# The order of the attention units: row block inside head, and one score product per step

## The chip, the cores and the metric

The kernel runs on one core of a Trainium2 chip. The metric is the device time of one execution in microseconds (us); lower is better.

## The reference

The reference is two transformer blocks on 256 tokens of width 2048, batch 1, in float32. The change lies in the second block, in its sparse attention, whose input projection and attention read

```python
h = rms_norm_2(x, ln_mix_pre[l])
z = h @ w_in[l]
q, kv, nsa_gl, u, merge_logits = jnp.split(z, splits, axis=-1)
q = q.reshape(b, s, NSA_HEADS, HEAD_DIM)               # 16 heads of 64
kv = kv.reshape(b, s, 6, NSA_GROUPS, HEAD_DIM)         # 4 groups of keys and values
a = nsa_attention(q, kv[:, :, 0], ..., kv[:, :, 5], nsa_gl, ...)
# in nsa_attention, for each block of 128 queries and each head, float32:
s_s = einsum(q, k_sel) * scale + bias;  p_s = masked_softmax(s_s);  o_s = p_s @ v_sel
s_w = einsum(q, k_win) * scale + bias;  p_w = masked_softmax(s_w);  o_w = p_w @ v_win
out = gate_c * o_c + gate_s * o_s + gate_w * o_w
```

With 256 tokens every selection block and the whole window are in reach, so both softmaxes run over all keys up to the query: 128 keys for the first block of queries (r = 0) and 256 for the second (r = 1).

## The kernel before

All engines are programmed by hand: each has one list of instructions, in an order written out in Python, and they meet through semaphores. There is no scheduler.

**Weights.** A weight slab of 1 MB (4 tiles of 128 rows by up to 512 columns) goes by DMA into one of four `raw` buffers. ScalarE writes its rounded part to `wh` (`hi`), VectorE the remainder to `wl` (`lo`, L1722), two buffers each, and TensorE multiplies it as 24 float32r matmuls: 2 row blocks, 4 tiles, 3 products (`slab_mm`, L1098 to L1100).

**The stage of the change.** Forty-eight steps m. In step m TensorE multiplies slab m of the second block's input projection (`z2_slab`); the attention on columns already there runs between the slabs. There are 32 units, one for each head and query block; unit u starts in step u + 12 (`STEP_U`). In one step TensorE does, in this order: the slab; the scores of a unit (`scores`, L1537, one float32 product of Q transposed with the selected and the window keys together, 2 x 128 columns out for r = 0 and 2 x 256 for r = 1); the transposes of the probabilities of unit u - 2 (`prob_turn`, L1572, 2 blocks for r = 0, 4 for r = 1); the products with the values for unit u - 3 (`weighted`, L1589 and L1591).

A head has 64 dimensions, so the score product contracts over 64 partitions. `par` says which half: the queries and keys of a unit with par = 0 lie in partitions 0 to 63, those with par = 1 in 64 to 127 (`QT`, `KT2`). A float32 product is two instructions for TensorE, here called passes.

VectorE does in step m: `biased(u)` (adds the bias L2217 by the helper at L1720, row maximum L2220, its negative L2221), then `lo` of slab m + 2, then `gathered(u - 3)` (L2273 to L2284). ScalarE does `hi` of slab m + 2, `prob_out(u - 2)` (L948) and the exponentials of unit u (`probs`).

Before the change the units go in the order (r, par) = (0,0), (0,1), (1,0), (1,1) for each i. The scores of two units stand back to back in every second step:

```python
if 0 <= u < UNITS and u % 2 == 0:
    scores(u)
    scores(u + 1)
```

The unit with even u writes bank 2, the one with odd u bank 3.

Of the kernel before, what the change touches and what calls it, by code (L numbers as in the profile page):

```python
# [23 lines left out]
SEQ, D, RB = 256, 2048, 2  # L24
# [37 lines left out]
UNITS = NH * RB  # L62
# [8 lines left out]

def unit(u):

    i, r, par = u // 4, (u % 4) // 2, u % 2
    return 8 * (i // 4) + 4 * par + i % 4, i, par, r

XH, XD = 4, 128
# [130 lines left out]
def build(nc, A, out):  # L208
    ctx = ExitStack()
    with ctx:  # L210
        named = {}

        def S(name):
            if name not in named:
                named[name] = ctx.enter_context(nc.semaphore(name))
            return named[name]
# [147 lines left out]
        def QT(i, par, r):  # L364

            c0 = 256 * (i % 4) + P * r
            return Z2[HD * par:HD * par + HD, i // 4, c0:c0 + P]

        def KT2(g, n):

            return Z2[HD * (g % 2):HD * (g % 2) + HD, g // 2, Z2_KV + 512:Z2_KV + 1536].rearrange("p (b c) -> p b c", b=2)[:, :, 0:n]
# [203 lines left out]
        def _(act):  # L575
            st = Slabs()

            def f(out_, in_, func, name, **kw):
                act.activation(out_, in_, func, **kw).then_inc(S(name), 1)  # L579
# [361 lines left out]

            def prob_out(u):

                nb = 2 + 2 * unit(u)[3]
                act.wait_ge(S("n_turned"), u + 1)
                if u >= 2:
                    act.wait_ge(S("n_pv"), u - 1)
                f(pT[:, u % 2, 0:nb * P], PB[4][:, 0:nb * P], ACT.Copy, "npT_out")  # L948
# [8 lines left out]
            for m in range(STEPS):  # L957
# [32 lines left out]
                u = m - STEP_U  # L990
# [62 lines left out]
        def _(pe):  # L1053
# [407 lines left out]
            def z2_slab(m):  # L1461

                n, s = 4 + m // 4, m % 4
                evacuated = RB * (CHUNK0["zin2"] + n - 1)
                if n == 4 and s == 0:
                    pe.wait_ge(chunk_out, evacuated)
                slab_mm((0, 1), ALL[4 * s:4 * s + 4], Z2_PARTS[n // Z2N][1], s == 0, s == 3, half=s == 3,
                        row_free=evacuated if s == 0 and n > 4 else None)

            def raw_turn(b):  # L1470

                pe.wait_ge(chunk_out, RB * (CHUNK0["zin2"] + 4))
                if b == 3:
                    pe.wait_ge(S("pe_out"), 1)
                for k in range(2):
                    for r in range(RB):
                        c0 = Z2_KV + KVW * (b // 2) + HD * (2 * (b % 2) + k)
                        cols = slice(SEQ * k + P * r, SEQ * k + P * r + P)
                        pe.transpose(PB[4 + b][0:HD, cols], Z2[:, r, c0:c0 + HD], ident)
                        mm = pe.matmul(PB[4 + b][HD:2 * HD, cols], Z2[:, r, c0:c0 + HD], ident, start=True, stop=True)  # L1480
                mm.then_inc(S("raw_turned"), 1)

            def hidden_w1(k):

                pe.wait_ge(S(f"w1_in{k}"), 32)
                pe.wait_ge(S("raw_out"), 4)
                for l in range(CS):
                    mm = pe.matmul(PB[4 + k][:, 0:NG * NCMP].rearrange("p (g n) -> p g n", g=NG), w1s[k][:, l, :],
                                   rawT[k][:, :, l:l + CS * (NCMP - 1) + 1:CS], start=l == 0, stop=l == CS - 1)
                mm.then_inc(S("w1_used"), 1)  # L1490

            def compressed():

                pe.wait_ge(S("gelued"), 2)
                for par in range(2):
                    mm = pe.matmul(PB[6][HD * par:HD * par + HD, 0:NG // 2 * NCMP].rearrange("p (q n) -> p q n", q=NG // 2),
                                   w2s[:, 0, :], hidT[:, 0, :].rearrange("p (q g n) -> p g q n", g=2, n=NCMP)[:, par, :, :],
                                   start=True, stop=True)
                mm.then_inc(S("kc_done"), 1)
                for g in range(NG):  # L1500
                    mm = pe.matmul(PB[7][0:NCMP, HD * g:HD * g + HD], hidT[:, 1, NCMP * g:NCMP * g + NCMP], w2s[:, 1, :],
                                   start=True, stop=True)
                mm.then_inc(S("kc_done"), 1)

            def query_turn(p):

                pe.wait_ge(S("kc_out"), 2)
                for j in range(4):
                    i = 4 * p + j
                    for r in range(RB):  # L1510
                        cols = slice(SEQ * (i % 2) + P * r, SEQ * (i % 2) + P * r + P)
                        low, high = (Z2[:, r, HD * h:HD * h + HD] for h in (8 * p + j, 8 * p + 4 + j))
                        pe.transpose(PB[4 + i // 2][0:HD, cols], low, ident)
                        mm = pe.matmul(PB[4 + i // 2][HD:2 * HD, cols], high, ident, start=True, stop=True)
                    if i % 2:
                        mm.then_inc(S("nq_turned"), 1)

            def key_turn():

                pe.wait_ge(S("nq_out"), 4)  # L1520
                pe.wait_ge(chunk_out, RB * (CHUNK0["zin2"] + 6))
                for p in range(2):
                    for b in range(2):
                        for r in range(RB):
                            c0 = Z2_KV + 512 * (1 + b) + P * p
                            mm = pe.transpose(PB[4 + p][:, SEQ * b + P * r:SEQ * b + P * r + P], Z2[:, r, c0:c0 + P], ident)
                    mm.then_inc(S("nk_turned"), 1)

            def scores(u):

                h, i, par, r = unit(u)
                g, nk = h // HPG, P * (r + 1)
                if u == 0:
                    pe.wait_ge(S("nk_out"), 4)
                elif u % 2 == 0:
                    pe.wait_ge(S("n_added"), u)
                pe.matmul(PB[2 + u % 2][:, 0:2 * nk].rearrange("p (b n) -> p b n", b=2), QT(i, par, r), KT2(g, nk),  # L1537
                          start=True, stop=True).then_inc(S("n_scored"), 1)

            def cmp_scores(r):  # L1540

                pe.wait_ge(S("nq_out"), 4)
                n_c = (NCMP0, NCMP)[r]
                for u in (u for u in range(UNITS) if unit(u)[3] == r):
                    h, i, par, _ = unit(u)
                    c0 = 16 * (8 * r + i)
                    mm = pe.matmul(PB[7 - par][:, c0:c0 + n_c], QT(i, par, r), kcT[HD * par:HD * par + HD, h // HPG // 2, 0:n_c],
                                   start=True, stop=True)
                mm.then_inc(S("c_scored"), 1)
                if r:  # L1550
                    pe.wait_ge(S("spread"), 1)
                    pe.wait_ge(S("nk_out"), 4)
                    pe.matmul(PB[5][:, 0:NG * HD], spread[0:NCMP, :, :].rearrange("p k c -> p (k c)"),
                              vc[:, :, :].rearrange("p g n -> p (g n)"), start=True, stop=True).then_inc(S("vc_spread"), 1)
# [57 lines left out]
            for m in range(STEPS):  # L1612
                z2_slab(m)
                if m == STEP_PE:
                    pe.transpose(PB[7][:, 0:2 * CS], perow[:, :], ident[0:2 * CS, 0:2 * CS]).then_inc(S("pe_turned"), 1)
                if m in STEP_RAW:
                    raw_turn(2 * STEP_RAW.index(m))
                    raw_turn(2 * STEP_RAW.index(m) + 1)
                if m in STEP_W1:
                    hidden_w1(STEP_W1.index(m))  # L1620
                if m == STEP_KC:
                    compressed()
                if m in STEP_Q:
                    query_turn(STEP_Q.index(m))
                if m == STEP_K:
                    key_turn()
                if m in STEP_CS:
                    cmp_scores(STEP_CS.index(m))
                if m == STEP_CT:
                    cmp_turn()  # L1630
                u = m - STEP_U
                if 0 <= u < UNITS and u % 2 == 0:
                    scores(u)
                    scores(u + 1)
                if 0 <= u - LAG_T < UNITS:
                    prob_turn(u - LAG_T)
                if 0 <= u - LAG_PV < UNITS:
                    weighted(u - LAG_PV)
                for g in range(PG):
                    if STEP_POOL[g] == m and m < STEPS - 1:  # L1640
                        pool_mix(g)
# [765 lines left out]
```

## Time and profile before

| | |
|---|---|
| median of 3 runs | 2881.47 us |
| lowest and highest | 2875.43 and 2883.66 us |
| the profiled execution | 2875.43 us |
| its span, first to last instruction | 2873.7 us |
| busy share: TensorE, VectorE, ScalarE | 93%, 58%, 40% |
| mean granted TensorE clock | 0.959 |
| the 32 units' steps | from about 1569 to 1802 us |

In the profile PE is TensorE's matmuls, PEld its weight loads, DVE VectorE, ACT ScalarE, SP the engine that issues the DMAs. A line stands for an instruction or for several alike in a row (xN): start, duration, engine, line, output <- inputs. The durations of successive matmuls overlap, since they are pipelined; what a matmul costs is the time from its start to the start of the next one.

### The profile page before, as it was taken

The numbers are of one execution on the slowest core, as the hardware profiler recorded it, in microseconds if no ns is written. First come the engines' busy times: TensorE is split into PE (matmuls) and PEld (weight loads), VectorE is DVE, ScalarE is ACT, GpSimd is POOL, SyncE is SP. The second block draws the span as 40 slices with busy tenths as digits, with TensorE's granted clock in tenths as the row PEclk, the third lists the DMA queues.
The fourth block names the chain that finished last, engine by engine and source line by source line (L and its number), as shares of the span: only waits on it lengthen the run. The fifth ranks groups of instructions, "written<-read, shape, count | busy, mean of one in ns | idle before, by whom it ended". The sixth has DMA issues, their size and how long they took to land.

```text
span 2873.7 us, 31089 instructions
## 1 busy us (share of the span) xinstructions
PE 2668.5 (93%) x12240; PEld 2192.0 (76%) x12240; DVE 1666.6 (58%) x1704; ACT 1157.5 (40%) x1207; POOL 0.2 (0%) x4
## 2 busy tenths in 40 slices
PE   6899669969999999999899999899789999999997
PEld 5678457757888888887788888778667888888886
DVE  7778566855666455555543666464554555555556
ACT  4333345443333333333433544434553333333333
POOL 0000000000000000000000000000000000000000
PEclk8899779979999999999899999999999999999999
DMA  9889843936777555555473444455335555555553
GB/s 325 322 292 371 232 175 119 364 103 223 247 258 251 162 189 190 190 190 169 130 215 123 154 153 141 146 180 190 122 130 188 190 187 181 191 189 188 190 189 131
DMA packets 265649, 566.00 MB, mean 197 GB/s; under 512 B 9648, under 2 KB 52558, under 8 KB 256479
## 3 DMA queue, kind: packets, MB, share of 16 engines
q1 hardware_dynamic: 265566, 564.87, 58.6%
q8 instruction: 56, 0.92, 0.1%
q14 instruction: 27, 0.21, 0.0%
HBM read 559.59 MB, written 5.24 MB: 197 GB/s over the span
## 4 chain that ended last, share of the span: by engine, by line
PE 76%; DVE 10%; ACT 5%; DMA 4%; issue 4%; SPq 1%; DVEq 0%; ACTq 0%
PE bank L1098 23%; PE bank L1100 22%; PE bank L1099 22%; ACT wh L586 3%; DVE wl L1720 3%; DVE ACC L1874 2%; DMA raw<-in_w_in 2%; DVE ROWB L1720 1%; DMA raw<-in_w_out 1%; DMA raw<-in_w_ada 1%; PE bank L1069 1%; DVE X L1843 1%; PE bank L1172 1%; PE bank L1589 1%; DVE ACC L1741 1%
## 5 line engine op out<-in xcount | busy, mean ns | idle before, releaser
L1720 DVE TENSOR_TENSOR wl<-raw,wh 128x2048 fp32r<-128x2048 f32 (+2 forms) x430 | 974.7, 2267 | 934.0 <-ACT wh L586 933.5
L586 ACT ACTIVATE wh<-raw 128x2048 fp32r<-128x2048 f32 (+2 forms) x430 | 815.6, 1897 | 1262.4 <-PE bank L1100 1127.1
L1098 PE MATMUL bank<-wh,XTh 128*128 128x512 f32 (+2 forms) x2648 | 1045.1, 395 | 32.1 <-DVE wl L1720 27.1
L1099 PE MATMUL bank<-wl,XTh 128*128 128x512 f32 (+2 forms) x2648 | 1033.0, 390 | 0.0
L1100 PE MATMUL bank<-wh,XTl 128*128 128x512 f32 (+2 forms) x2648 | 1032.7, 390 | 0.0
L1098 PEld LDWEIGHTS bank<-wh,XTh 128*128 128x128 f32 x2648 | 504.2, 190 | 139.4 <-DVE wl L1720 28.3
L1100 PEld LDWEIGHTS bank<-wh,XTl 128*128 128x128 f32 x2648 | 503.3, 190 | 99.5
L1099 PEld LDWEIGHTS bank<-wl,XTh 128*128 128x128 f32 x2648 | 504.5, 191 | 95.1
L1098 PE MATMUL bank<-wh,HTh 128*128 128x512 f32 x704 | 276.8, 393 | 9.4 <-DVE HTl L1720 3.6
L1100 PE MATMUL bank<-wh,HTl 128*128 128x512 f32 x704 | 274.2, 389 | 0.0
L1099 PE MATMUL bank<-wl,HTh 128*128 128x512 f32 x704 | 274.0, 389 | 0.0
L1098 PEld LDWEIGHTS bank<-wh,HTh 128*128 128x128 f32 x704 | 132.1, 188 | 46.5 <-issue 14.4
L1100 PEld LDWEIGHTS bank<-wh,HTl 128*128 128x128 f32 x704 | 132.1, 188 | 27.9
L1099 PEld LDWEIGHTS bank<-wl,HTh 128*128 128x128 f32 x704 | 132.2, 188 | 26.6
L1720 DVE TENSOR_TENSOR ROWB<-ROWB,bank 128x512 f32<-128x512 f32 x176 | 112.6, 681 | 10.9 <-PE bank L1100 9.0
L1741 DVE SCALAR_TENSOR_TENSOR ACC<-raw,cT,ACC 128x2048 f32<-128x2048 f32 x45 | 105.7, 2349 | 4.7 <-DMA raw<-in_w_ada 1.1
L1874 DVE SCALAR_TENSOR_TENSOR ACC<-raw,cT,ACC 128x512 f32<-128x512 f32 x112 | 75.5, 747 | 0.0
L872 ACT ACTIVATE HTh<-bank 128x512 fp32r<-128x512 f32 x44 | 23.9, 595 | 90.4 <-PE bank L1417 90.4
L1069 PE MATMUL bank<-CON,X 128*128 128x128 f32 x96 | 19.8, 375 | 27.3 <-DVE X L1843 17.2
L1069 PEld LDWEIGHTS bank<-CON,X 128*128 128x128 f32 x96 | 15.8, 193 | 31.5 <-issue 18.3
L1737 DVE SCALAR_TENSOR_TENSOR ACC<-raw,cT,ACC 128x2048 f32<-128x2048 f32 x16 | 37.6, 2351 | 1.8 <-DVE wl L1720 0.9
L579 ACT ACTIVATE JUNK<-ROWB 128x512 f32<-128x512 f32 x40 | 24.9, 628 | 31.1 <-DVE ROWB L1720 31.1
(305 smaller groups left out, 1460.9 us busy)
## 6 DMA issues: line engine op xcount, KB each, us to landing
raw<-in_w_ada SPq DMA_DIRECT2D x96, 1024.0 KB, 6.6
raw<-in_w_ffn_gate SPq DMA_DIRECT2D x44, 1024.0 KB, 5.2
raw<-in_w_ffn_up SPq DMA_DIRECT2D x44, 1024.0 KB, 5.2
raw<-in_w_ffn_down SPq DMA_DIRECT2D x44, 1024.0 KB, 5.0
raw<-in_w_gate SPq DMA_DIRECT2D x44, 1024.0 KB, 5.2
raw<-in_w_up SPq DMA_DIRECT2D x44, 1024.0 KB, 5.1
raw<-in_w_down SPq DMA_DIRECT2D x44, 1024.0 KB, 5.1
raw<-in_w_in SPq DMA_DIRECT2D x32, 1024.0 KB, 5.1
```

The lines of the kernel that those rows point to most:

```text
L586: act.activation(wh[:, st.lin % 2, 0:width], raw[:, st.raw % 4, 0:width], ACT.Copy).then_inc(hi_made, 1)
L1069: mm = pe.transpose(PB[turn_bank(name, b)][:, SEQ * k + P * r:SEQ * k + P * r + P], src(r, 2 * b + k), ident)
L1098: pe.matmul(out_, hi_t[:, k, rows], w[0][:, q, :], start=first and q == 0, stop=False)
L1099: pe.matmul(out_, hi_t[:, k, rows], w[1][:, q, :], start=False, stop=False)
L1100: mm = pe.matmul(out_, lo_t[:, k, rows], w[0][:, q, :], start=False, stop=last and q == n - 1)
L1172: mm = pe.matmul(o, ACC[:, c0:c0 + P], ones[:, 0:1], start=q == 0 and par == 0, stop=par == 1, skip_group_check=True)
L1589: pe.matmul(PB[7][:, HD * b:HD * b + HD], pT[:, u % 2, P * blk_:P * blk_ + P], Z2[:, k, c0:c0 + HD], start=k == 0, stop=k == r)
L1720: return dve.tensor_tensor(out_, a, b, op)
L1737: ins = dve.scalar_tensor_tensor(ACC[:, :], w, cT[:, bass.ds(k0 + k, 1)], ACC[:, :], ALU.mult, ALU.add)
L1741: ins = dve.scalar_tensor_tensor(ACC[:, :], w, cT[:, k:k + 1], ACC[:, :], ALU.mult, ALU.add)
L1843: dve.scalar_tensor_tensor(x, y, nstat[:, j, 2, r:r + 1], x, ALU.mult, ALU.add).then_inc(S("x_added"), 1)
L1874: ins = dve.scalar_tensor_tensor(part, w, c, part, ALU.mult, ALU.add)
```

## The change

The unit order becomes (r, par) = (0,0), (1,0), (0,1), (1,1): the two query blocks of one head follow each other, so that even u always has r = 0 and odd u r = 1. The scores of one unit are issued in each of 32 steps instead of two units in each of 16, and each waits until the bias addition of the unit before is done. Two other places that depend on the order are rewritten for the new one. The products, their sizes and their number stay.

```diff
 def unit(u):
-    i, r, par = u // 4, (u % 4) // 2, u % 2
+    i, par, r = u // 4, (u % 4) // 2, u % 2
     return 8 * (i // 4) + 4 * par + i % 4, i, par, r
...
             def prob_out(u):
-                nb = 2 + 2 * unit(u)[3]
+                nb = 2 + 2 * (u % 2)
                 act.wait_ge(S("n_turned"), u + 1)
...
                 if u == 0:
                     pe.wait_ge(S("nk_out"), 4)
-                elif u % 2 == 0:
+                else:
                     pe.wait_ge(S("n_added"), u)
                 pe.matmul(PB[2 + u % 2][:, 0:2 * nk].rearrange("p (b n) -> p b n", b=2), QT(i, par, r), KT2(g, nk),
                           start=True, stop=True).then_inc(S("n_scored"), 1)
...
-                for u in (u for u in range(UNITS) if unit(u)[3] == r):
+                for u in range(r, UNITS, RB):
                     h, i, par, _ = unit(u)
...
                 u = m - STEP_U
-                if 0 <= u < UNITS and u % 2 == 0:
+                if 0 <= u < UNITS:
                     scores(u)
-                    scores(u + 1)
                 if 0 <= u - LAG_T < UNITS:
                     prob_turn(u - LAG_T)
```

## Rows read from the trace of the kernel before

**Rows 1.** The page: busy time of the engines.
```profile
PE 2668.5 (93%) x12240; PEld 2192.0 (76%) x12240; DVE 1666.6 (58%) x1704; ACT 1157.5 (40%) x1207; POOL 0.2 (0%) x4
```

**Rows 2.** Windows: stretch, length, busy of PE, PEld, DVE, ACT, POOL, clock, DMA share, GB/s.
```profile
1569.00:1802.00 233.00, 233.00 (x1200) 188.99 (x1201) 151.19 (x315) 114.76 (x210) 0.00 (x0) 1.00 0.49 155
1802.00:2200.00 398.00, 357.06 (x1632) 295.68 (x1632) 211.79 (x221) 186.20 (x213) 0.00 (x0) 0.95 0.46 155
2200.00:2873.00 673.00, 656.26 (x2919) 539.84 (x2918) 358.68 (x264) 251.10 (x173) 0.00 (x0) 0.99 0.56 182
```

**Rows 3.** Waits of PE from 1565 to 2010: who for whom, us, times, longest.
```profile
PE bank L1069 <- DVE XTl L1720: 6.3, 2, 5.7
...
PE bank L1098 <- DVE wl L1720: 2.0, 1, 2.0
```

**Rows 4.** PE timeline of a 4-step cycle: slab's end, scores, transposes, value products.
```profile
1592.48 0.39 PE L1100 MATMUL bank<-wh,XTl 128*128 128x512 f32 x1
1592.80 0.70 PE L1537 MATMUL bank<-Z 64*128 64x256 f32 x4
1593.43 0.65 PE L1572 MATMUL bank<-CON,nprob 128*128 128x128 f32 x4
1593.92 0.56 PE L1589 MATMUL bank<-Z,pT 128*128 128x64 f32 x4
...
1599.86 0.40 PE L1100 MATMUL bank<-wh,XTl 128*128 128x512 f32 x1
1600.10 0.60 PE L1572 MATMUL bank<-CON,nprob 128*128 128x128 f32 x4
1600.53 1.00 PE L1589 MATMUL bank<-Z,pT 128*128 128x64 f32 x8
...
1606.88 0.39 PE L1100 MATMUL bank<-wh,XTl 128*128 128x512 f32 x1
1607.20 1.13 PE L1537 MATMUL bank<-Z 64*128 64x512 f32 x4
1608.26 0.44 PE L1572 MATMUL bank<-CON,Z 128*128 128x128 f32 x2
1608.53 1.00 PE L1589 MATMUL bank<-Z,pT 128*128 128x64 f32 x8
...
1614.88 0.39 PE L1100 MATMUL bank<-wh,XTl 128*128 128x512 f32 x1
1615.11 0.38 PE L1572 MATMUL bank<-CON,Z 128*128 128x128 f32 x2
1615.33 0.56 PE L1589 MATMUL bank<-Z,pT 128*128 128x64 f32 x4
...
1621.58 0.70 PE L1537 MATMUL bank<-Z 64*128 64x256 f32 x4
```

**Rows 5.** Line 1537, from 1607.19 to 1607.60 us: durations, first and last start.
```profile
L1537 PEld LDWEIGHTS bank<-Z x4: 183/184/186, 1607.2 to 1607.3; 64*128 64x128 f32 x4
L1537 PE MATMUL bank<-Z x2: 693/693/693, 1607.2 to 1607.2; 64*128 64x512 f32 x2
```

**Rows 6.** PE timeline where two whole-height score products of 256 columns follow.
```profile
2066.41 1.03 PE L1686 MATMUL bank<-xkT,xqT 128*128 128x256 f32 x4
2067.28 0.60 PE L1695 MATMUL bank<-CON,xp 128*128 128x128 f32 x4
```

**Rows 7.** PE timeline of a single float32 product with few rows.
```profile
1561.60 0.69 PE L1553 MATMUL bank<-vc,spread 15*128 15x256 f32 x2
1562.23 0.75 PE L1098 MATMUL bank<-wh,XTh 128*128 128x454 f32 x1
```

**Rows 8.** DVE timeline after the pair at 1607.20 us.
```profile
1608.36 0.69 DVE L1720 TENSOR_TENSOR nprob<-bank,REL 128x512 f32<-128x512 f32 x1 [2.39 <-PE bank L1537]
...
1609.88 2.28 DVE L1720 TENSOR_TENSOR wl<-raw,wh 128x2048 fp32r<-128x2048 f32 x1
...
1612.93 0.60 DVE L2284 SCALAR_TENSOR_TENSOR REL<-bank,nwt,REL 128x64 f32<-128x64 f32 x2
```

## The prediction

> **What bounds the kernel now.** I read the page first. TensorE is busy 93% of the span, the next engine 58% [rows 1]. That is an average over many stages, so I went to the stage of the change, steps 12 to 46 of the 48, from 1569 to 1802 us. The windows view shows TensorE busy in all 233.00 of its 233 us, VectorE in 151.19 and ScalarE in 114.76, at a granted clock of 1.00, which is the level of 2.4 GHz, and with the DMA engines at 0.49 [rows 2]. The view of waits, opened wider (1565 to 2010 us), has few entries for TensorE, and the two lines shown come after this stage: the waits at L1069 (6.3 us) and the one at L1098 (2.0 us) belong to the turn from attention to the pooling and merge products that follows slab 47 [rows 3]; asked for 1569 to 1802 alone, the view names no wait of a matmul at all. So here TensorE's own queue of work sets the time. What is added to it is paid in full, and what is taken from or given to the other engines costs nothing until one of them makes TensorE wait.
>
> Next I read TensorE's timeline through one cycle of four steps, which covers both kinds of pair and both steps without scores [rows 4]. The reader should look at starts. The last matmul of a slab (L1100) starts, and the next thing starts 0.24 or 0.23 us later where no scores are between (1599.86 to 1600.10, 1614.88 to 1615.11). With a pair of scores between, it is 0.95 us for r = 0 (1592.48 to 1593.43) and 1.38 us for r = 1 (1606.88 to 1608.26).
>
> Last, the row of L1537 over the first 0.4 us of a pair [rows 5]. Two score matmuls start at 1607.2, and both last 693 ns. They are the first passes of two different units: one uses the partitions 0 to 63 of the array, the other 64 to 127. They run side by side. All four passes of the pair are done in 1.06 us [rows 4].
>
> **The change part by part.**
>
> *The pairs are broken up.* The new order and the one score product per step leave no second product with the other half beside it. The question is what one unit costs alone. The whole cost of a pair first. For r = 0: 0.95 - 0.24 = 0.71 us, and the four transposes behind it take 0.49 us to the next start (1593.43 to 1593.92) where they take 0.43 without scores ahead (1600.10 to 1600.53), so 0.77 us. For r = 1: 1.38 - 0.23 = 1.15 us, and the two transposes behind take 0.27 (1608.26 to 1608.53) against 0.22 (1615.11 to 1615.33), so 1.20 us [rows 4].
>
> A lone unit, from below: it must stream its own columns. Four passes of 256 columns over all 128 rows, two products, take 0.87 us (2066.41 to 2067.28) [rows 6], so one product of 256 columns takes 0.435 us and one of 512 columns 0.87 us. From above: a lone unit costs what a pair costs, 0.77 and 1.20 us, as though the second product had been free. I take the upper value, for two reasons. The pair's own time splits as one product's streaming and a constant: 0.63 = 0.435 + 0.195 and 1.06 = 0.87 + 0.19. Nothing in it is left for the second product, and a constant alike at both sizes looks like the change from full height to half height and back. And the trace has a lone float32 product of 256 columns that uses few rows (15): from its start to the next matmul it takes 0.63 us (1561.60 to 1562.23) [rows 7], the same as the pair of L1537.
>
> There were 8 pairs of each kind, 16 in all; there will be 16 lone units of each kind. Each pair that becomes two lone units adds one more such cost: 8 x 0.77 + 8 x 1.20 = 6.2 + 9.6 = 15.8 us. By the lower price of the extra product the sum is 8 x 0.435 + 8 x 0.87 = 10.4 us.
>
> The Trainium skill, page "TensorE: Matmul & The Clock Gate", section "Part 3: Packing small matmuls — row/col tiling", says that a weight load overlaps with matmuls in flight only where the row groups differ. By it the second pass of a lone product could not hide its weight load, and the extra products would cost more than a pair does. The rival on that load below prices it from a row.
>
> *The added waits.* Scores of odd u now wait for the bias addition of unit u - 1. Behind them in TensorE's queue stand the transposes and value products of the step and then slab m + 1. That addition begins 0.1 us after the scores of its own unit end (1608.26 to 1608.36) and takes 0.69 us [rows 8], in the step before, with a whole slab between. I cost it at nothing. The cover is that slab; without it, 0.8 us in each of 16 steps.
>
> *VectorE's work moves.* Before, the addition and maximum for odd u ran early, in idle time, since their scores had been made a step ahead. Now every unit's follow its own scores, ahead of `lo` for slab m + 2. What is late next is `lo`, and then `gathered`, which frees bank 7 for the value products of the next unit. Priced by the heaviest case, an r = 1 unit: scores start at 1607.20, `lo` ends at 1609.88 + 2.28 = 1612.16, `gathered` at 1612.93 + 0.60 = 1613.53, 6.33 us after the scores' start [rows 4, 8]. TensorE's next value products started at 1615.33, 8.13 us after it [rows 4]. In the new order the step behind odd u has four transposes for two (+0.16 to +0.2), value products of an r = 0 unit in place of r = 1 (x4 for x8; the eight take 0.44 us longer, by their durations of 1.00 and 0.56), and the lone r = 0 scores of the next step (+0.77): about 8.6 us. A margin of 2.3 us stays, where before the least was 1.8. The slab after that needs `lo` later still. So nothing is added.
>
> *ScalarE and the DMA queue.* The number of exponentials and copies is the same; r = 0 and r = 1 only alternate. SP's queue waits for all 32 scores before it loads the band matrices. The last scores move from step 42 to 43, but the slab issued just ahead of that wait needs a `lo` which VectorE does in step 43 behind the last unit's addition, so it is later anyway. The compressed scores keep their order under the rewritten loop. All of this costs nothing.
>
> The sum: + 15.8 us. The profiled execution took 2875.43 us with a span of 2873.7, so it would become 2891.2. It is the lowest of the three runs; the median is 6.0 us higher. For the median I forecast 2881.47 + 15.8 = 2897 us.
>
> **The rivals.**
>
> *The second pass's weight load shows.* A load of L1537 lasts 184 ns [rows 5]. Were it paid once in each of the 16 extra products, the sum would be 15.8 + 16 x 0.184 = 18.7 us, or 2900 us. Against it: in [rows 6] four passes follow at 0.22 us each with a load for each, and so hide them. It shifts the size, not the sign; I hold it inside the main case.
>
> *No change.* The extra time of TensorE would be taken up by idle time that it has anyhow. For it: the 6.3 us wait at L1069 that follows the stage [rows 3]. Against it: that wait starts only after slab 47 has been multiplied, so it moves along, and inside the stage nothing is idle. It would give 2881 us, within 0.3%. 1 in 10.
>
> *VectorE becomes the bound.* If its chain grows by more than the 2.3 us, value products wait for bank 7. Each 0.5 us past that point in the 16 odd steps adds 8 us: 2881.47 + 15.8 + 8 = 2905. Against it stands the margin just worked out. 6 in 100.
>
> *Faster, by the clock.* From 1802 to 2873 us the granted clock averages 0.95 and 0.99 [rows 2]. With the two levels of 1.2 and 2.4 GHz, that is 398 x 0.05 x 2 = 40 us and 673 x 0.01 x 2 = 13 us at the lower one, which costs half of it, 27 us. All later work starts 16 us later, and could meet the falls of the clock otherwise. It decides once more than 15.8 us of the 27 come back; if all did, the time would be 2881.47 + 15.8 - 27 = 2870. Against it: the falls stand at stretches where TensorE waits for others (357.06 busy us of 398), and these stay. 4 in 100.
>
> **How the numbers follow.** The main case has 80 in 100. Its own range is from the lowest run and the lower price, 2875.43 + 10.4 = 2886, to the highest run and the weight load, 2883.66 + 18.7 = 2902. With the start of VectorE's case the range is 2885 to 2906. The main case and VectorE's are slower by over 0.3% (8.6 us, about what a measurement of this kernel can tell from no change), but for a few in 100 at the low edge; so slower 0.84, same 0.12, faster 0.04.
>
> **What the profile would show.** L1537's rows would read x2, not x4, in 32 places, with about 0.63 and 1.06 us from their start to the next matmul. The four-step cycle, 28.78 us from one r = 0 pair to the next (1592.80 to 1621.58, where the next begins), would become 30.8 us, and the stage 249 us instead of 233. TensorE would still be busy all through it. Wrong would be: a lone product well under 0.63 or 1.06 us (then the constant belonged to the pair, and the sum falls towards 10.4); a wait of L1589 for L2284 or of L1098 for `lo`; or a gain outside the stage at a higher granted clock.

## The result, and the profile after

The changed kernel takes 2897.87 us (median of 5 runs, 2889.93 to 2903.53) against 2881.47 us before. The ratio is 1.0059, with a 95% interval from 1.0044 to 1.0074: slower by 13 to 21 us. (Each ratio in this document is taken against runs of the kernel before that were made together with those of the kernel measured, so it can differ slightly from the quotient of two medians.)

The profiled execution after has a span of 2896.5 us, 22.8 us more than that of before. To see where they are, two starts on TensorE are enough: that of the first score product (L1537) and that of the first pooling product (L1606), which follows the attention's last step. What lies between them is called the stage below. In the view of a line the columns are the count, durations in ns (least, median, greatest), and first and last start in us. The kernel before:

```profile
L1537 PE MATMUL bank<-Z x64: 376/534/693, 1568.9 to 1780.4; 64*128 64x256 f32 x32, 64*128 64x512 f32 x32
L1606 PE MATMUL bank<-Z x16: 378/379/435, 1802.2 to 1819.2; 128*128 128x256 f32 x16
```

The kernel after:

```profile
L1537 PE MATMUL bank<-Z x64: 376/534/693, 1575.1 to 1809.2; 64*128 64x256 f32 x32, 64*128 64x512 f32 x32
L1606 PE MATMUL bank<-Z x16: 378/379/435, 1824.3 to 1841.2; 128*128 128x256 f32 x16
```

The stage took 1802.2 - 1568.9 = 233.3 us and now takes 1824.3 - 1575.1 = 249.2: 15.9 us more. The durations of the score products are the same to the nanosecond, and so is their number. Of the other 6.9 us, 6.2 lie ahead of the stage, where both kernels do the same work. Windows of before and after over that stretch (the columns as in [rows 2]):

```profile
0.00:1568.90 1568.90, 1422.04 (x6493) 1167.38 (x6493) 944.84 (x905) 605.47 (x612) 0.20 (x4) 0.94 0.65 220
```

```profile
0.00:1575.10 1575.10, 1429.10 (x6492) 1173.57 (x6492) 943.49 (x901) 605.86 (x612) 0.20 (x4) 0.93 0.65 219
1575.10:1824.30 249.20, 249.15 (x1204) 192.80 (x1203) 153.47 (x320) 114.62 (x210) 0.00 (x0) 1.00 0.46 145
```

The mean clock there reads 0.93 for 0.94; 6 us are 0.4% of the stretch, so the rounded rows allow for it without proving it. It need not be the change's: in the kernels below, all with the same work ahead of the stage, the first score product starts anywhere from 1568.8 to 1579.3 us. That is why the experiments below are read by the length of the stage first, and by the runs' times second.

In the stage TensorE is still busy all the time, 249.15 of 249.20 us, at a granted clock of 1.00. VectorE and ScalarE do in 249 us what they did in 233. TensorE's timeline after, two steps, answers to [rows 4]:

```profile
1608.63 0.39 PE L1100 MATMUL bank<-wh,XTl 128*128 128x512 f32 x1
1608.95 1.12 PE L1537 MATMUL bank<-Z 64*128 64x512 f32 x2
1610.00 0.66 PE L1572 MATMUL bank<-CON,nprob 128*128 128x128 f32 x4
1610.49 0.56 PE L1589 MATMUL bank<-Z,pT 128*128 128x64 f32 x4
...
1616.41 0.39 PE L1100 MATMUL bank<-wh,XTl 128*128 128x512 f32 x1
1616.73 0.70 PE L1537 MATMUL bank<-Z 64*128 64x256 f32 x2
1617.36 0.44 PE L1572 MATMUL bank<-CON,Z 128*128 128x128 f32 x2
```

The score rows say x2 where they said x4, yet they last as long. From 1608.95 to the next start it is 1.05 us (1.06 for the pair), from 1616.73 it is 0.63 us (0.63 for the pair). One product now takes the time that two took.

### The profile page after: what moved, and what is told of

Its sections match the earlier page's. It is cut to its first block, busy times and chain, and to the rows that moved or that the text cites. A ratio compares the mean times of both kernels' runs of the same rounds, so it can differ in the third digit from the quotient of the medians.

```text
span 2896.5 us, 31089 instructions
## 1 busy us (share of the span) xinstructions
PE 2691.6 (93%) x12240; PEld 2201.6 (76%) x12240; DVE 1667.4 (58%) x1704; ACT 1158.0 (40%) x1207; POOL 0.2 (0%) x4
## 4 chain that ended last, share of the span: by engine, by line
PE 75%; DVE 10%; DMA 5%; ACT 5%; issue 4%; SPq 1%; DVEq 0%; ACTq 0%
PE bank L1098 22%; PE bank L1100 22%; PE bank L1099 22%; ACT wh L586 4%; DVE wl L1719 3%; DMA raw<-in_w_in 2%; DVE ACC L1873 2%; DVE ROWB L1719 1%; DMA raw<-in_w_out 1%; DMA raw<-in_w_ada 1%; PE bank L1069 1%; PE bank L1537 1%; DMA raw<-in_w_xkv 1%; DVE X L1842 1%; PE bank L1589 1%
## 5 line engine op out<-in xcount | busy, mean ns | idle before, releaser
L1100 PE MATMUL bank<-wh,XTl 128*128 128x512 f32 (+2 forms) x2648 | 1034.4, 391 | 0.0
L1099 PE MATMUL bank<-wl,XTh 128*128 128x512 f32 (+2 forms) x2648 | 1034.0, 390 | 0.0
L1100 PEld LDWEIGHTS bank<-wh,XTl 128*128 128x128 f32 x2648 | 503.7, 190 | 99.8
L1099 PEld LDWEIGHTS bank<-wl,XTh 128*128 128x128 f32 x2648 | 505.4, 191 | 95.8
L1100 PE MATMUL bank<-wh,HTl 128*128 128x512 f32 x704 | 274.2, 390 | 0.0
L1099 PE MATMUL bank<-wl,HTh 128*128 128x512 f32 x704 | 274.0, 389 | 0.0
L1100 PEld LDWEIGHTS bank<-wh,HTl 128*128 128x128 f32 x704 | 132.1, 188 | 27.8
L1099 PEld LDWEIGHTS bank<-wl,HTh 128*128 128x128 f32 x704 | 132.2, 188 | 26.8
L1069 PEld LDWEIGHTS bank<-CON,X 128*128 128x128 f32 x96 | 15.8, 193 | 31.5 <-issue 18.3
```

The costliest lines, as they stand in the source:

```text
L1069: mm = pe.transpose(PB[turn_bank(name, b)][:, SEQ * k + P * r:SEQ * k + P * r + P], src(r, 2 * b + k), ident)
L1099: pe.matmul(out_, hi_t[:, k, rows], w[1][:, q, :], start=False, stop=False)
L1100: mm = pe.matmul(out_, lo_t[:, k, rows], w[0][:, q, :], start=False, stop=last and q == n - 1)
```

## The experiments

Each experiment starts from the kernel before or from the changed one. The stage of each is worked out as above, from the first starts of its own two lines, in its one profiled execution; added lines in a kernel shift the numbers behind them by up to three. The granted clock of the stage reads 1.00 in all of them but two, the one with six VectorE reductions and the one with a wait inside the pair. A table at the end of this section has them all.

**One product per step, in the old order.** The edit, to the kernel before:

```diff
-                elif u % 2 == 0:
+                else:
                     pe.wait_ge(S("n_added"), u)
...
-                if 0 <= u < UNITS and u % 2 == 0:
+                if 0 <= u < UNITS:
                     scores(u)
-                    scores(u + 1)
```

> The unit order of before, but one score product per step, each behind a wait for the addition before it. Measure: the stage, from the first L1537 to the first pooling product, 233.3 us before and 249.1 after the change. Theory (two products in opposite halves of the array overlap only when they stand together; a lone one costs what a pair costs): stage 249.1, time of before + 15.8, some 2897. Rival, the order (query blocks alternating step by step load TensorE, VectorE and ScalarE otherwise): since the order is the old one, stage 233.3 and the time of before.

Measured: 2898.04 us, ratio 1.0061 (1.0044 to 1.0077), stage 1828.4 - 1579.3 = 249.1 us.

```profile
L1537 PE MATMUL bank<-Z x64: 376/534/693, 1579.3 to 1813.4; 64*128 64x256 f32 x32, 64*128 64x512 f32 x32
L1606 PE MATMUL bank<-Z x16: 377/379/435, 1828.4 to 1845.3; 128*128 128x256 f32 x16
```

The whole loss is there with the order of before. The alternation of query blocks costs nothing by itself.

**The new order, in couples.** Two units are issued together again, but in the new order they use the same half of the array (a couple, where a pair uses both halves). The edit, to the changed kernel:

```diff
-                else:
+                elif u % 2 == 0:
                     pe.wait_ge(S("n_added"), u)
...
-                if 0 <= u < UNITS:
+                if 0 <= u < UNITS and u % 2 == 0:
                     scores(u)
+                    scores(u + 1)
```

> The changed order, but units u and u + 1 issued together in every second step, as before the change. The two are now the two query blocks of one head and use the same half of the array. Theory: they don't overlap; the second streams behind the first and only the change of height is saved, 1.97 us for two lone units against 0.09 + 0.19 + 0.435 + 0.87 + 0.05 = 1.64, 16 times: stage 243.8, time of before + 10.5, some 2892. Rival, one product per step (more waits, more changes of height) is what costs: back to 233.3 and the time of before. Rival, the order is what costs: 249.1.

Measured: 2892.77 us, ratio 1.0048 (1.0029 to 1.0067), stage 1812.3 - 1568.8 = 243.5 us. TensorE's timeline of it:

```profile
1608.90 0.39 PE L1100 MATMUL bank<-wh,XTl 128*128 128x512 f32 x1
1609.22 1.55 PE L1537 MATMUL bank<-Z 64*128 64x256 f32 x4
1610.70 0.44 PE L1572 MATMUL bank<-CON,Z 128*128 128x128 f32 x2
```

The four passes (the row carries the shape of its first; two have 256 columns, two 512) take 1.48 us, where the pair of two 512-column products took 1.06. Two products in the same half queue: 0.435 + 0.87 + 0.19 = 1.495. So issuing in twos is not enough; the halves must be opposite ones. This kernel splits the loss in two: 243.5 - 233.3 = 10.2 us come from the lost overlap alone, and the other 249.2 - 243.5 = 5.7 us from having scores in 32 steps instead of 16.

**The pair parted.** In the kernel before, the transposes are put between the two products of a pair:

```diff
                 if 0 <= u < UNITS and u % 2 == 0:
                     scores(u)
-                    scores(u + 1)
                 if 0 <= u - LAG_T < UNITS:
                     prob_turn(u - LAG_T)
+                if 0 <= u < UNITS and u % 2 == 0:
+                    scores(u + 1)
```

> The kernel of before with the transposes of the step moved between the two score products of a pair; order, waits and number per step stay. Theory: without standing together they don't overlap and the height changes twice, so each costs as a lone one: stage 249, time of before + 15.8. Rival, the number of steps with scores and their waits are what counts: 233.3 and the time of before.

Measured: 2896.33 us, ratio 1.0060 (1.0039 to 1.0081), stage 1820.8 - 1571.8 = 249.0 us. The timeline:

```profile
1612.13 1.12 PE L1537 MATMUL bank<-Z 64*128 64x512 f32 x2
1613.19 0.44 PE L1572 MATMUL bank<-CON,Z 128*128 128x128 f32 x2
1613.55 1.12 PE L1537 MATMUL bank<-Z 64*128 64x512 f32 x2
1614.61 1.10 PE L1589 MATMUL bank<-Z,pT 128*128 128x64 f32 x8
```

Here the order, the step, the waits and the halves are those of before, and only the transposes of one unit (two blocks in the rows shown, four behind an r = 0 product) stand between. Each product again costs what the pair did, 1.06 us. This is the narrowest form of the change, and it has all of its cost but 0.2 us. It takes away both the overlap and the shared entry into half height; the couples above tell the two apart.

**One more product, in the other half and in the same half.** To the changed kernel a score product is added ahead of each but the first, 31 in all, of the same size, into bank 6, which is free then; nothing reads it. In one kernel it uses the other half of the array, in the next the same half (`par` and `g` for `1 - par` and `g ^ 1`):

```diff
+                if u:
+                    pe.matmul(PB[6][:, 0:2 * nk].rearrange("p (b n) -> p b n", b=2), QT(i, 1 - par, r), KT2(g ^ 1, nk),
+                              start=True, stop=True)
                 pe.matmul(PB[2 + u % 2][:, 0:2 * nk].rearrange("p (b n) -> p b n", b=2), QT(i, par, r), KT2(g, nk),
```

> The changed kernel, with one more score product of the same size ahead of each but the first, 31 in all, in the other half of the array and into a bank that is free (its result is not used). Theory: it runs beside the lone one and costs nothing: stage 249 to 250. Rival, a lone product is cheaper than half a pair and the pair's time was shared: 15 x 0.435 + 16 x 0.87 = 20.4 us more, stage 269.5.

> The changed kernel with one more score product of the same size ahead of each but the first, 31 in all, this time in the same half of the array. Theory (in one half products queue, each for the time of its columns, 0.435 us or 0.87 us): 15 x 0.435 + 16 x 0.87 = 20.4 us more, stage 249.1 + 20.4 = 269.5. Rival, the rule of the skill's page TensorE: Matmul & The Clock Gate that a weight load overlaps with matmuls in flight only where the row groups differ: its 62 loads of 0.184 us come on top, 11.4 us, stage 281.

Measured, other half: 2893.47 us in one run, stage 1819.4 - 1570.1 = 249.3 us. TensorE's timeline, the extra product at L1538 and the real one at L1540:

```profile
1603.83 0.69 PE L1538 MATMUL bank<-Z 64*128 64x512 f32 x1
1603.84 0.69 PE L1540 MATMUL bank<-Z 64*128 64x512 f32 x1
1604.37 0.59 PE L1538 MATMUL bank<-Z 64*128 64x512 f32 x1
1604.37 0.59 PE L1540 MATMUL bank<-Z 64*128 64x512 f32 x1
1604.89 0.66 PE L1575 MATMUL bank<-CON,nprob 128*128 128x128 f32 x4
```

The passes of the two products start within 0.01 us of each other, and all is done after 1.06 us. Thirty-one products more cost 0.1 us in the stage.

Measured, same half: 2922.80 us in one run, stage 1847.1 - 1577.5 = 269.6 us, 20.4 us over the changed kernel.

```profile
1613.85 1.12 PE L1538 MATMUL bank<-Z 64*128 64x512 f32 x2
1614.82 1.02 PE L1540 MATMUL bank<-Z 64*128 64x512 f32 x2
1615.77 0.66 PE L1575 MATMUL bank<-CON,nprob 128*128 128x128 f32 x4
```

Here one product follows the other, 1.92 us in all against 1.05 for one: 0.87 us for 512 columns, as [rows 6] gave. The weight loads of the added products are hidden, though they go to the half that is computing: 249.2 + 20.4 = 269.6 us is the streaming of their columns and nothing else, and 62 loads paid in full would have made it 281. The Trainium skill, "TensorE: Matmul & The Clock Gate", section "Part 3: Packing small matmuls — row/col tiling", says that a load overlaps with matmuls in flight only where the row groups differ. The measurement decides against it here.

**VectorE's margin.** Reductions of 128x512 are added in each odd step of the changed kernel, between the unit's maximum and `lo`, six in one kernel and two in another:

```diff
                     biased(u)
+                    if u % 2:
+                        for k in range(6):
+                            dve.tensor_reduce(PADT[:, 6 * (u // 2) + k:6 * (u // 2) + k + 1], X[:, 0, 0:512], AX.X, ALU.max)
                 step_lo(m + 2)
```

> The changed kernel with six more VectorE reductions of 128x512 in each odd step, between the unit's maximum and the low part of the next slab (some 0.72 us each from start to start, 4.3 us in all; their results are not used). The margin of VectorE's chain is 1599.92 (end of the last weighting) to 1602.27 (the value products that wait for it), 2.35 us. Theory: what exceeds it delays TensorE, 4.3 - 2.35 = 2.0 us in each of 16 steps, so the stage is some 31 us longer, 280, and L1589 waits for the last weighting. Rival, the next step's idle time takes it up: 249.

> The same with two more reductions, 1.44 us. It lies under the margin of 2.35 us: stage 249. Rival, VectorE is already what sets the odd steps after the change: 16 x 1.44 = 23 us more, 272.

Measured: with two, 2897.12 us in one run, stage 1821.8 - 1572.7 = 249.1 us, nothing. With six, 2932.58 us, ratio 1.0168 (1.0139 to 1.0197), stage 1855.6 - 1577.9 = 277.7 us. The waits of TensorE in the kernel with six, and one odd step of VectorE and what follows on TensorE:

```profile
PE bank L1590 <- DVE REL L2284: 18.6, 15, 1.9
PE bank L1099 <- DVE wl L1720: 1.1, 1, 1.1
```

```profile
1652.41 3.65 DVE L2304 TENSOR_REDUCE padt<-X 128x1 f32<-128x512 f32 x6
```

```profile
1658.14 0.44 PE L1573 MATMUL bank<-CON,Z 128*128 128x128 f32 x2
1659.78 1.08 PE L1590 MATMUL bank<-Z,pT 128*128 128x64 f32 x8 [1.20 <-DVE REL L2284]
```

The six take 3.56 us (1652.41 to 1655.97, where `lo` starts), not 4.3. Less the margin of 2.35 that leaves 1.2 us, and TensorE waits 1.20. The mechanism and the margin are right. The stage grew by 28.5 us, though, and these fifteen waits sum to 18.6. The rest can be found in the timeline and in the window over the stage:

```profile
1577.90:1855.60 277.70, 257.96 (x1204) 197.20 (x1203) 207.41 (x416) 116.31 (x210) 0.00 (x0) 0.98 0.41 132
```

From the start of the transposes to that of the value products it is 1.64 us in the step above, where it was 0.27 without a wait. Over the fifteen steps (1.62 to 1.64 us in fourteen, 2.32 in the last) this makes 21.0 us more, waits included. The value products themselves then take some 0.07 us longer (0.91 for 0.84), 1.0 us in all, and one wait for `lo` at L1099 adds 1.1. The clock, as in the last section, reads 0.98: 277.7 x 0.02 x 2 = 11 us at the lower level, which costs 5.6. Together 28.7 us, which agrees with 28.5 as far as a clock rounded to 0.01 allows.

**The wait without its cover.** The kernel before, with pairs, but the second product of a pair also waits for the addition of the first unit:

```diff
-                elif u % 2 == 0:
+                else:
                     pe.wait_ge(S("n_added"), u)
```

> The kernel of before, pairs and order kept, with one wait added: the second product of a pair waits until the bias addition of the first unit is done, so no slab covers the wait. Theory: TensorE stands in the middle of each pair for 0.1 us and the addition (0.43 us for the first query block, 0.69 for the second) and some 0.1 us to start again, and the products no longer overlap: 15.8 + 8 x 0.63 + 8 x 0.9 = 28 us more, stage 261. Rival, the wait costs nothing as it did in the changed kernel, only the overlap is lost: + 15.8, stage 249.

Measured: 2913.82 us, ratio 1.0106 (1.0079 to 1.0133), stage 1842.3 - 1573.5 = 268.8 us, 35.5 us over before, where 28 had been expected.

```profile
1618.66 1.12 PE L1537 MATMUL bank<-Z 64*128 64x512 f32 x2
1620.56 1.12 PE L1537 MATMUL bank<-Z 64*128 64x512 f32 x2 [0.79 <-DVE nprob L1720]
1621.62 0.69 PE L1572 MATMUL bank<-CON,Z 128*128 128x128 f32 x2
1622.10 1.81 PE L1589 MATMUL bank<-Z,pT 128*128 128x64 f32 x8
```

In this pair, of the second query block, the wait has the size forecast: 1.90 us from the first product to the second, 0.84 over 1.06. In pairs of the first block, whose addition is shorter, it is 1.21 us, 0.58 over 0.63. What was not forecast is the last row, eight value products in 1.81 us that took 1.00 before [rows 4]. They wait for nobody; the clock had fallen (last section).

**Four products together.** From the kernel before: from unit 4 on, the pair for the first query block and the pair for the second are issued in one step of four, into banks 2, 3, 5 and 6. The banks are renamed alike where VectorE reads them (not shown), and TensorE waits for the additions only ahead of each group.

```diff
+def NBANK(u): return 2 + u % 2 if u < 4 else (2, 3, 5, 6)[u % 4]
...
-                elif u % 2 == 0:
+                elif u == 2 or u % 4 == 0:
                     pe.wait_ge(S("n_added"), u)
-                pe.matmul(PB[2 + u % 2][:, 0:2 * nk].rearrange("p (b n) -> p b n", b=2), QT(i, par, r), KT2(g, nk),
+                pe.matmul(PB[NBANK(u)][:, 0:2 * nk].rearrange("p (b n) -> p b n", b=2), QT(i, par, r), KT2(g, nk),
...
-                if 0 <= u < UNITS and u % 2 == 0:
-                    scores(u)
-                    scores(u + 1)
+                if 0 <= u < UNITS and u % (4 if u >= 4 else 2) == 0:
+                    for v in range(u, u + (4 if u >= 4 else 2)):
+                        scores(v)
```

> The kernel of before with four score products issued together every fourth step from unit 4 on: the pair for the first query block, then the pair for the second, into banks 2, 3, 5 and 6. Theory: both pairs still overlap, and a change of height and the gaps around it are saved 7 times. From the coupled products of the changed order, (249.2 - 243.5) / 16 = 0.36 us each: stage 233.3 - 2.5 = 230.8, time some 2.5 us less than before, 0.1%, which the runs can't tell from none. Rival, something waits for the products that come up to two steps early or for the banks: stage 233 or more.

Measured: 2880.83 us, ratio 0.9995 (0.9981 to 1.0008), stage 1804.4 - 1573.3 = 231.1 us.

```profile
1625.92 1.56 PE L1538 MATMUL bank<-Z 64*128 64x256 f32 x8
1627.41 0.66 PE L1573 MATMUL bank<-CON,nprob 128*128 128x128 f32 x4
```

Eight passes take 1.49 us; the couple of the second experiment took 1.48 us for four. The stage is 2.2 us shorter than before; the runs' times can't show it, since their interval includes no change.

| kernel | score products | stage, us | expected |
|---|---|---|---|
| before | pairs in opposite halves | 233.3 | |
| changed | lone | 249.2 | 249 |
| old order | lone | 249.1 | 249.1 |
| new order | couples in the same half | 243.5 | 243.8 |
| pair parted by transposes | lone | 249.0 | 249 |
| changed, one more each | other half | 249.3 | 249 to 250 |
| changed, one more each | same half | 269.6 | 269.5 |
| changed, VectorE + 2 | lone | 249.1 | 249 |
| changed, VectorE + 6 | lone | 277.7 | 280 |
| pair with a wait inside | parted by the wait | 268.8 | 261 |
| fours | two pairs together | 231.1 | 230.8 |

## Why the prediction was right

- **The bound.** TensorE has no wait of a matmul in the stage after either, and is busy 249.15 of 249.20 us. What was added to its queue came out in full.
- **The price of a lone product.** The sum took the upper of two prices, that a lone unit costs what a pair costs. The timeline after shows 0.63 and 1.05 us for 0.63 and 1.06, the extra product in the other half costs nothing, and the one in the same half costs the lower price, 0.435 and 0.87 us. So both ends were real prices, of two different edits: the lower one is that of a further product in the same half without a change of height. The 10.4 us at the low end are what the couples in the same half cost, measured as 10.2.
- **The sum.** 15.8 us were forecast for the stage and 15.9 measured. The four-step cycle, forecast at 30.8 us, is twice 1616.73 - 1601.37 = 15.36, so 30.7. The forecast time, 2897, stands against 2897.87, but that closeness is partly luck: the five runs spread over 13.6 us, and the profiled executions differ by another 6.9 us outside the stage. The sum is borne out by the stage.
- **The added waits cost nothing**, as forecast: the old order with one product per step, which has them too, takes no more than the changed one, and TensorE shows none. The price given for the case without cover, 0.8 us in each of 16 steps, was read from the wrong addition, though nothing hung on it. In the new order the unit ahead of an odd one has r = 0, whose addition takes 0.43 us and not 0.69, and the pair with a wait shows both: a wait of 0.79 us behind an r = 1 unit and of 0.52 behind an r = 0 unit. The total there was higher than forecast for a reason the prediction did not have, the clock.
- **VectorE's margin** was worked out as 2.3 us; in the trace after it is 2.35, from the end of `gathered` at 1599.32 + 0.60 = 1599.92 to the value products at 1602.27. Added work below it was free, above it came out as a wait of the difference. The rival was possible but far off. The rows after:

```profile
1599.32 0.60 DVE L2283 SCALAR_TENSOR_TENSOR REL<-bank,nwt,REL 128x64 f32<-128x64 f32 x2
```

```profile
1601.37 0.70 PE L1537 MATMUL bank<-Z 64*128 64x256 f32 x2
...
1602.27 1.00 PE L1589 MATMUL bank<-Z,pT 128*128 128x64 f32 x8
```

- **The second weight load** (18.7 us in the sum): not paid, since the stage grew by 15.9. Loads hide behind the passes of the same half.
- **No change, and faster by the clock:** behind the stage the executions differ by 1072.2 - 1071.5 = 0.7 us, at a clock of 0.98 in both, so neither was anything taken up nor given back there.
- **Where the cost lies.** The parted pair, with the order, waits and steps of before, has it all but 0.2 us. That singles out one thing, that two products in opposite halves stood together. It was worth two savings at once: the overlap (10.2 us, by the couples) and one entry into half height for two products (5.7 us).

## What to carry to other kernels

Where a product contracts over half of the partitions, look at the starts of its matmuls: if two start together, the second is free, and whatever comes between them (here a slab, transposes or a wait) costs a full product. When units are reordered for balance or simplicity, keep the half that alternates as the innermost index, and issue the two halves back to back; of the loss here, the order alone would have brought back nothing, and standing together in one half brought back 5.7 of 15.9 us. And where one engine is busy all through a stage, its cost can be summed from start-to-start times to a few tenths of a us, far finer than whole runs can tell.

## What the runs showed of the hardware

**A change of height has a constant price.** A full-height stream that goes to half height and back loses 0.19 us on top of the columns at both sizes, and some 0.14 us around (0.77 - 0.63 and 1.20 - 1.06). Merging two such visits into one, the couples saved (249.2 - 243.5) / 16 = 0.36 us a time, and the fours (233.3 - 231.1) / 7 = 0.31. The weight loads (PEld) after show where the time may go:

```profile
1608.40 0.19 PEld L1100 LDWEIGHTS bank<-wh,XTl 128*128 128x128 f32 x1
1608.94 0.29 PEld L1537 LDWEIGHTS bank<-Z 64*128 64x128 f32 x2 [0.35 <-issue]
```

Inside the slab a load starts a whole matmul ahead: that of the last L1100 at 1608.40, its matmul at 1608.63. The first load of the scores starts only at 1608.94, with its matmul at 1608.95. The constant is as long as one load, 184 ns [rows 5], so it could be that one load standing uncovered. No run separates this from another cause.

**The clock fell in the two stages where TensorE had waits.** In the stages of before and after the granted clock was 1.00. In the pair with a wait inside, the waits were 0.5 to 0.8 us each, but for the first of 1.5. Windows over its stage (columns as in [rows 2]):

```profile
1573.00:1842.00 269.00, 257.61 (x1203) 201.46 (x1202) 151.65 (x318) 115.46 (x210) 0.00 (x0) 0.96 0.42 135
...
1620.00:1640.00 20.00, 18.92 (x75) 14.67 (x76) 10.71 (x23) 8.26 (x15) 0.00 (x0) 0.83 0.31 95
```

TensorE was busy 257.61 of 269 us, yet the mean clock over the stage was 0.96. With levels of 1.2 and 2.4 GHz that is 269 x 0.04 x 2 = 21.5 us at the lower one, which costs half, 10.8 us: without it the stage would be 258, near the 261 expected. The stretch from 1620 to 1640 us has one fall. While it lasts, the matmuls of the slab follow at 0.43 us instead of 0.23:

```profile
1625.94 0.63 PE L1099 MATMUL bank<-wl,XTh 128*128 128x512 f32 x1
1626.37 0.63 PE L1100 MATMUL bank<-wh,XTl 128*128 128x512 f32 x1
...
1629.16 0.39 PE L1099 MATMUL bank<-wl,XTh 128*128 128x512 f32 x1
1629.39 0.39 PE L1100 MATMUL bank<-wh,XTl 128*128 128x512 f32 x1
```

What stood ahead of that fall were half-height products, a wait of 0.79 us and small transposes. The products and transposes alone did not bring it about. The parted pair has the same ones in its stage, in slightly another order and with no wait, and kept a clock of 1.00:

```profile
1571.80:1820.80 249.00, 249.00 (x1203) 194.01 (x1203) 151.28 (x316) 115.01 (x210) 0.00 (x0) 1.00 0.46 146
```

So the waits have a part in it, and a short wait can cost more than its length. Not each wait does: windows of 0.5 us over the stage show five falls for sixteen waits, each within 2.5 us of the start of a product that had waited, and 20.5 us at the lower level in all. With six VectorE reductions there are three falls for fifteen waits, 10.3 us in all. Why these waits and not the others stays open.
